# Negated scores, one fused join of a head's two maps, heads between scores, and the conv module's slots projected first

## The chip, the cores and the metric

The kernel runs as one program on one core of a Trainium2 chip. The metric is the device time of that core in microseconds (us), the median of several runs. In the profile's words PE is TensorE (PEld its weight loads), DVE is VectorE, ACT is ScalarE, POOL is GpSimd and SP is SyncE, whose queue issues the loads of weights.

## What is computed

256 tokens of width 1024 go through two layers of a first block and then through a second block (latent attention, pooling and two passes over 128 expert slots). The change lies in the mixer of the first block's two layers, of which this matters:

```python
for l in range(DEPTH):                      # 2 layers
    h = rms_norm(x, pre_mix_w[l])
    u = h @ w_in[l]
    (u_conv, dq, dk, dv, gqkv, gz, b_f, b_b, a_f, a_b) = jnp.split(u, offs, axis=-1)
    y_conv = conv_module(u_conv, ...)       # a * sigmoid(g), 31 taps, layer norm, silu
    y_diff = diff_attention(dq, dk, dv, ...)
    y_delta = gated_deltanet(gqkv, gz, b_f, b_b, a_f, a_b, ...)   # 3 taps, silu, chunks
    y = jnp.concatenate([y_conv, y_diff, y_delta], axis=-1) @ w_out[l]
    ...
# diff_attention: 6 heads, two maps each (12 maps), 128 queries x 256 keys twice
s = jnp.einsum("bqmd,bkmd->bmqk", q_blk, kf)
p = jax.nn.softmax(s - slopes[:, None, None] * dist, axis=-1)
a = p[:, :, 0] - lam * p[:, :, 1]
o = rms_norm(jnp.einsum("bhqk,bkhe->bqhe", a, vf), subln_w, eps=1e-5) * (1.0 - lambda_init)
```

## The kernel before

Each engine has one instruction stream, and semaphores tie them together. The order of a layer's mixer is written out by hand, in the same order in each engine's function: `pe_layer`, `dve_layer`, `act_layer` and `pool_layer`.

TensorE writes its results into four PSUM banks in rotation. The list in `layer_jobs` names every use of a bank and the engine that empties it. `J.give` on TensorE takes the next bank and waits until the job four places earlier has been read; `J.take` on the reader waits until the bank is filled; `J.evac` waits until a job has been read.

The weights come in slots of 1 MB through a ring of four, loaded by SyncE in the order in which TensorE uses them; `project(i, key)` multiplies slot 4 + i with the activations, 16 matmuls of 256 columns for each of a slot's two tiles of 128 channels. Before the change the order is: the untransposed slots ("zb", "dv"), the five "s" slots (the channels of the delta net's q, k and v; the fifth holds one tile), "cg" and "ca" (gate and value of the conv module), then small sums of the log decays ("gc", "gl", four "gr"), then "d" 0, the sums for the l2 norm ("l2"), "d" 1 and "d" 2 (q and k of the attention).

VectorE waits for the last "s" slot (evacuated by ScalarE) and runs the short convolution of three taps: nine TENSOR_SCALAR (L997) and eighteen SCALAR_TENSOR_TENSOR (L999) over 256 elements, all from SBUF to SBUF. Behind it in VectorE's queue stand the product for `cpad`, the conv module's padded input (L1008), the copy of "gc" and the four "gr". ScalarE waits for the short convolution (signal `sconv`), then applies silu and square, loads another table and reads "gl". GpSimd waits for the reading of "ca" and then works off the conv module's 31 taps, each a TENSOR_TENSOR multiply (L1416) and a TENSOR_TENSOR add (L1418) over 512 elements: 20 of them, then after the last head's output a square (`od2`), 3 taps, a reciprocal root, twelve scalings of keys and values, and the last 8 taps.

The scores follow: for each of 12 maps TensorE fills a bank (L559), VectorE adds the distance term (L1036), takes the maximum (L1039) and negates it (L1040), and ScalarE exponentiates with the row sums as a by-product (L1285). Only when all 12 are through VectorE come the six heads: reciprocal of the sums (L1048), factor lambda (L1049), scaling of the first map (L1051, two operations), adding the second map (L1054, two operations), and TensorE transposes the joined map ("ar", L593) and multiplies with v ("av", L570), ScalarE copying both out. The blocks "kk" and "qk" (L580) of the delta net are filled around the last head, and from there a long algebra of 64x64 blocks (L608) runs between TensorE, VectorE (L1067, L1070, L1082, L1086) and ScalarE.

Of the kernel before, what the change touches and what calls it, by code (L numbers as in the profile page):

```python
# [18 lines left out]
S = 256  # L19
TB = S // P  # L20
# [152 lines left out]
def layer_jobs():  # L173
    j = [(("h", i), "act" if i % 2 == 0 else "dve") for i in range(4)]
    j += [(("zb", tb), "act") for tb in range(TB)] + [(("dv", tb), "act") for tb in range(TB)]
    j += [(("s", i), "act") for i in range(5)]
    j += [("cg", "act"), ("ca", "dve"), ("gc", "dve"), ("gl", "act")]
    j += [(("gr", g), "dve") for g in range(GRP)] + [(("d", 0), "act")]
    j += [(("l2", i), "act") for i in range(3)]
    j += [(("d", i), "act") for i in range(1, 3)]  # L180
    j += [(("sc", m), "dve") for m in range(NMAP)]
    for h in range(DH + 1):
        if h >= DH - 1:
            j += [((("kk", "qk")[h - (DH - 1)], hp), "dve") for hp in range(2)]
# [157 lines left out]
def plan_memory(nc, ctx, k):  # L342
# [137 lines left out]
def pe_layer(k, pe, lay):  # L480
# [22 lines left out]
    def project(i, key):  # L503
# [8 lines left out]
        m.then_inc(J.filled, 1)  # L512
        rel.owe()

    for i in range(5):
        project(i, ("s", i))
    project(5, "cg")
    project(6, "ca")

    pe.wait_ge(k.const_loaded, 16)  # L520
    wait(k.g_ready)
# [30 lines left out]
    project(9, ("d", 2))  # L552

    J.evac(pe, ("d", 2), lay)
    for m_ in range(NMAP):
        b = J.give(pe, ("sc", m_), lay)
        r = (m_ % 4) * DD
        for qb in range(TB):
            m = pe.matmul(ps[b][:, qb * S:(qb + 1) * S], k.qkd[r:r + DD, m_ // 4, qb * P:(qb + 1) * P],  # L559
                          k.qkd[r:r + DD, 3 + m_ // 4, :], start=True, stop=True)  # L560
            if qb == 0:
                rel.pay(m)
        m.then_inc(J.filled, 1)
# [22 lines left out]
    for h in range(DH):  # L586
        if h == DH - 1:
            chunk_pairs("kk", 3)
        wait(k.attn_ready, h + 1)
        b = J.give(pe, ("ar", h), lay)  # L590
        for qb in range(TB):
            for kb in range(TB):
                m = pe.transpose(ps[b][:, kb * S + qb * P:kb * S + (qb + 1) * P],  # L593
                                 k.prob[:, 2 * h, qb, kb * P:(kb + 1) * P], c["ident"])
        m.then_inc(J.filled, 1)
        if h:
            attend(h - 1)
# [361 lines left out]
def dve_layer(k, v, lay):  # L959
# [28 lines left out]
    st.link(v.tensor_scalar(k.beta[:, :, :], k.beta[:, :, :], 1.0, None, ALU.add))  # L988
    st.link(v.reciprocal(k.beta[:, :, :], k.beta[:, :, :]))

    J.evac(v, ("s", 4), lay)
    for tap in range(3):
        for i in range(9):
# [8 lines left out]
            else:  # L1002
                st.done(m)
        st.settle()

    J.evac(v, "cg", lay)
    b = J.take(v, "dve", "ca", lay)
    v.tensor_tensor(k.cpad[:, :, PADC:PADC + S], shaped(ps[b][:, :], 2, S), k.csig[:, :, :], ALU.mult).then_inc(J.read["dve"], 1)  # L1008
# [24 lines left out]
    slopes = alibi(DH)  # L1033
    for m_ in range(NMAP):
        b = J.take(v, "dve", ("sc", m_), lay)
        v.scalar_tensor_tensor(k.prob[:, m_, :, :], k.dist[:, :, :], -slopes[m_ // 2], shaped(ps[b][:, :], TB, S),  # L1036
                               ALU.mult, ALU.add).then_inc(J.read["dve"], 1)
        J.evac(v, ("sc", m_), lay)
        st.link(v.tensor_reduce(k.mx[:, m_, :], k.prob[:, m_, :, :], AX.X, ALU.max))  # L1039
        v.tensor_scalar(k.mx[:, m_, :], k.mx[:, m_, :], -1.0, None, ALU.mult).then_inc(k.sc_max.sem, 1)  # L1040
    wait(k.gc_exp)
    v.tensor_tensor(k.beg[:, :, :], k.beta[:, :, :], k.eg[:, :, :], ALU.mult).then_inc(k.beg_ready.sem, 1)
# [3 lines left out]
    for h in range(DH):  # L1046
        wait(k.sc_exp, 2 * h + 2)
        st.link(v.reciprocal(k.ssum[:, 2 * h:2 * h + 2, :], k.ssum[:, 2 * h:2 * h + 2, :]))  # L1048
        st.link(v.tensor_scalar(k.ssum[:, 2 * h + 1, :], k.ssum[:, 2 * h + 1, :], k.lam[:, 5:6], None, ALU.mult))  # L1049
        for qb in range(TB):  # L1050
            st.done(v.tensor_scalar(k.prob[:, 2 * h, qb, :], k.prob[:, 2 * h, qb, :], k.ssum[:, 2 * h, qb:qb + 1], None, ALU.mult))  # L1051
        st.settle()
        for qb in range(TB):
            m = v.scalar_tensor_tensor(k.prob[:, 2 * h, qb, :], k.prob[:, 2 * h + 1, qb, :], k.ssum[:, 2 * h + 1, qb:qb + 1],  # L1054
                                       k.prob[:, 2 * h, qb, :], ALU.mult, ALU.add)
            st.done(m) if qb == 0 else m.then_inc(k.attn_ready.sem, 1)
    by_dir = lambda M, hp: M.rearrange("p (d m h) j -> p d m h j", d=2, h=2)[:, :, :, hp, :]
    for name, to, E in (("kk", k.A, k.EB), ("qk", k.AQ, k.E)):
        for hp in range(2):
# [159 lines left out]
def act_layer(k, a, lay):  # L1219
# [30 lines left out]
    a.activation(k.negA[:, :], k.row[:, R_ALOG:R_ALOG + 12], ACT.Exp).then_inc(k.gate_exp.sem, 1)  # L1250
    wait(k.lam_arg)
    a.activation(k.lam[:, 2:4], k.lam[:, 0:2], ACT.Exp).then_inc(k.lam_exp.sem, 1)
    for i in range(5):
        n = 1 if i == 4 else 2
        copy(("s", i), k.raw[:, 2 * i:2 * i + n, 1:S + 1], lambda t, n=n: shaped(t[:, 0:n * S], n, S))
    copy("cg", k.csig[:, :, :], lambda t: shaped(t[:, :], 2, S), ACT.Sigmoid)
    wait(k.sconv)
    sa.link(a.activation(k.sT[:, :, :], k.sT[:, :, :], ACT.Silu))
    a.activation(k.sq[:, :, :], k.sT[:, 0:6, :], ACT.Square).then_inc(k.sq_ready.sem, 1)
# [22 lines left out]
    for m_ in range(NMAP):  # L1282
        wait(k.sc_max, m_ + 1)
        for qb in range(TB):
            m = a.activation(k.prob[:, m_, qb, :], k.prob[:, m_, qb, :], ACT.Exp, bias=k.mx[:, m_, qb:qb + 1],  # L1285
                             accum_out=k.ssum[:, m_, qb:qb + 1])
            sa.done(m) if False else m.then_inc(k.sc_exp2.sem if qb == 0 else k.sc_exp.sem, 1)

    def out_head(h):
        copy(("av", h), k.od[:, :, h * HD:(h + 1) * HD], lambda t: shaped(t[:, 0:2 * HD], 2, HD))  # L1290

    for h in range(DH):
        copy(("ar", h), k.ATd[h % 2][:, :, :], lambda t: shaped(t[:, :], TB, S))
        if h:
            out_head(h - 1)
    out_head(DH - 1)
    def stack(key, M, g):
        copy(key, M[:, GH * g:GH * g + GH, :], lambda t: shaped(t[:, 0:BLOCKS], GH, CHUNK))
# [98 lines left out]
def pool_layer(k, p, lay):  # L1397
# [26 lines left out]
    x_rstd(1)  # L1424
    p.wait_ge(k.const_loaded, 16)
    J.evac(p, "ca", lay)
    conv_taps(range(0, 20))
    J.evac(p, ("av", DH - 1), lay)
    p.tensor_tensor(k.od2[:, :, :], k.od[:, :, :], k.od[:, :, :], ALU.mult).then_inc(k.od_sq.sem, 1)
    conv_taps(range(20, 23))  # L1430
    wait(k.od_ss)
    pool_rsqrt(k, p, sp, k.onorm[:, :], k.inv_hd, k.eps5, k.od_rstd)
    wait(k.beg_ready)
# [1 line left out]
    for dr in range(2):  # L1435
        for tb in range(TB):
            for src, dst, f in ((k.Kn, k.kbg, k.beg), (k.Kn, k.kdec, k.ekd), (k.Vn, k.vb, k.beta)):
# [3 lines left out]
                    m.then_inc(k.kv_scaled.sem, 1)  # L1441
                else:
                    sp.done(m)
    conv_taps(range(23, CONV_W))
    J.evac(p, ("ao", 3), lay)
    p.tensor_tensor(k.o2[:, :, :], k.o[:, :, :], k.o[:, :, :], ALU.mult).then_inc(k.o_sq.sem, 1)
    wait(k.o_ss)
# [1117 lines left out]
def layer_slots(i, l):  # L2565
# [80 lines left out]
```

## Time and profile before

| | us |
|---|---|
| median of 3 runs | 3168.43 |
| lowest, highest | 3165.46, 3171.89 |
| the profiled execution | 3174.81 |
| its span | 3172.8 |
| TensorE busy | 2939.2 (93%) |
| VectorE busy | 2045.8 (64%) |
| ScalarE busy | 1096.8 (35%) |
| GpSimd busy | 227.4 (7%) |
| mean granted TensorE clock | 0.948 of full |

The times are those of whole executions; the span is what the profiler saw between the first and the last instruction of one further execution. Busy shares are means over stages of very different kinds: the expert passes, which fill most of the span, have TensorE busy nearly throughout, and the two mixers, of some 300 us each, don't. All GpSimd work of note lies in the two mixers.

### The profile page before, as it was taken

How to read it: one execution, taken by the hardware profiler on the slowest of the kernel's cores; microseconds unless marked ns; L12 is line 12 of the kernel's file. 1: busy time of each engine (PE TensorE's matmuls, PEld its weight loads, DVE VectorE, ACT ScalarE, POOL GpSimd, SP SyncE). 2: the span in 40 equal slices, each digit the busy share in tenths (PEclk: the TensorE clock that was granted, in tenths of full speed). 3: DMA queues.
4: the chain of work that ended last, by engine and by line, in shares of the span. 5: the costliest groups of instructions: out<-in, count | busy, mean ns of one | idle time of the engine just before them, and what ended most of it. 6: DMA issues, size and time to landing. Idle time of an engine off the chain costs nothing.

```text
span 3172.8 us, 50021 instructions
## 1 busy us (share of the span) xinstructions
PE 2939.2 (93%) x19336; PEld 2496.4 (79%) x19340; DVE 2045.8 (64%) x3676; ACT 1096.8 (35%) x1741; POOL 227.4 (7%) x208
## 2 busy tenths in 40 slices
PE   8896999977799998989999999998898999999997
PEld 6684897867499745879899999885688989999986
DVE  1863885485388242599766666674289966666677
ACT  2321553241255230123444444441012344444443
POOL 0651000362100000000000000000000000000000
PEclk9797999977899998999999999998899999999999
DMA  5100884400388212442355555654353145445564
GB/s 208 65 17 13 321 327 148 173 15 15 145 328 302 90 50 97 169 153 79 136 183 185 185 185 185 221 199 151 133 173 131 68 174 181 182 184 184 185 239 152
DMA packets 77555, 502.31 MB, mean 158 GB/s; under 512 B 9072, under 2 KB 9456, under 8 KB 20592
## 3 DMA queue, kind: packets, MB, share of 16 engines
q1 hardware_dynamic: 71520, 481.72, 41.6%
q10 hardware_dynamic: 5904, 18.71, 1.6%
q8 instruction: 97, 1.59, 0.2%
q14 instruction: 34, 0.28, 0.0%
HBM read 487.82 MB, written 12.58 MB: 158 GB/s over the span
## 4 chain that ended last, share of the span: by engine, by line
PE 63%; DVE 9%; issue 1%; ACT 0%; DMA 0%; POOL 0%; DVEq 0%; ACTq 0%; POOLq 0%
PE bank L776 18%; PE bank L788 18%; PE bank L818 8%; PE bank L1814 4%; PE bank L1768 4%; PE bank L1823 4%; PE bank L1631 2%; PE bank L1651 1%; DVE sb L2039 1%; DVE sb L2032 1%; PE bank L1847 1%; DVE sb L2033 1%; DVE sb L2036 1%; DVE sb L2029 1%; DVE sb L2071 1%; DVE sb L2069 1%
## 5 line engine op out<-in xcount | busy, mean ns | idle before, releaser
L788 PE MATMUL bank<-peer_pass_high,peer_pass_hidden 128*128 128x512 f32 x1344 | 452.4, 398 | 0.0
L776 PE MATMUL bank<-peer_pass_high 128*128 128x256 f32 x1344 | 383.6, 285 | 13.8 <-DVE ring_r L863 13.8
L776 PE MATMUL bank<-peer_pass_high,ring_r 128*128 128x256 f32 x1344 | 385.8, 287 | 0.0
L776 PE MATMUL bank<-hT_r,peer_pass_high 128*128 128x256 f32 x1344 | 381.4, 284 | 0.0
L863 DVE TENSOR_TENSOR ring_r<-ring,peer_pass_high 128x1024 fp32r<-128x1024 f32 x168 | 205.8, 1225 | 194.1 <-ACT peer_pass_high L1356 194.1
L788 PEld LDWEIGHTS bank<-peer_pass_high,peer_pass_hidden 128*128 128x128 f32 x1344 | 253.9, 189 | 53.7
L776 PEld LDWEIGHTS bank<-peer_pass_high 128*128 128x128 f32 x1344 | 257.5, 192 | 22.7 <-issue 14.8
L1356 ACT ACTIVATE peer_pass_high<-ring 128x1024 fp32r<-128x1024 f32 x168 | 178.3, 1061 | 270.5 <-DMA ring<-in_experts 269.7
L788 PE MATMUL bank<-ring_r,peer_pass_hidden 128*128 128x512 f32 x672 | 267.4, 398 | 0.0
L776 PEld LDWEIGHTS bank<-hT_r,peer_pass_high 128*128 128x128 f32 x1344 | 257.9, 192 | 7.0
L776 PEld LDWEIGHTS bank<-peer_pass_high,ring_r 128*128 128x128 f32 x1344 | 257.4, 192 | 0.0
L1370 ACT ACTIVATE sb<-bank 128x256 f32<-128x256 f32 x232 | 89.4, 386 | 398.5 <-PE bank L776 398.5
L818 PE MATMUL bank<-peer_pass_high,peer_pass_hidden 128*128 128x512 f32 x704 | 225.0, 400 | 0.0
L867 DVE TENSOR_TENSOR ring_r<-ring,peer_pass_high 128x1024 fp32r<-128x1024 f32 x168 | 204.7, 1218 | 4.4 <-ACT peer_pass_high L1361 4.2
L1789 PE MATMUL bank<-sb,ring 128*128 128x256 f32 x896 | 193.7, 379 | 0.0
L1789 PEld LDWEIGHTS bank<-sb,ring 128*128 128x128 f32 x896 | 170.1, 190 | 23.0
L875 DVE TENSOR_TENSOR sb<-sb 128x256 f32<-128x256 f32 x168 | 104.7, 623 | 127.4 <-ACT sb L1370 127.4
L1361 ACT ACTIVATE peer_pass_high<-ring 128x1024 fp32r<-128x1024 f32 x168 | 175.7, 1046 | 7.9 <-PE bank L788 7.9
L788 PE MATMUL bank<-ff_high,ff_hidden 128*128 128x512 f32 x512 | 171.7, 397 | 2.2 <-DVE ff_hidden L872 2.2
L818 PEld LDWEIGHTS bank<-peer_pass_high,peer_pass_hidden 128*128 128x128 f32 x704 | 132.9, 189 | 32.7 <-issue 0.5
L2270 POOL TENSOR_SCALAR sb<-sb 128x2 f32<-128x2 f32 x4 | 1.9, 464 | 2120.1 <-DVE sb L1909 2120.1
L776 PE MATMUL bank<-ff_high 128*128 128x256 f32 x512 | 146.9, 287 | 5.8 <-DVE ring_r L863 5.8
(345 smaller groups left out, 5890.4 us busy)
## 6 DMA issues: line engine op xcount, KB each, us to landing
ring<-in_experts SPq DMA_DIRECT2D x256, 1024.0 KB, 4.8
ring<-in_w SPq DMA_DIRECT2D x139, 1024.0 KB, 4.9
sb<-in_w_mod SPq DMA_DIRECT2D x48, 1024.0 KB, 6.8
spill<-sb ACTq DMA_DIRECT2D x22, 512.0 KB, 6.5
sb<-spill SPq DMA_DIRECT2D x44, 256.0 KB, 5.1
sb<-in_ln ACTq DMA_DIRECT2D x8, 512.0 KB, 4.8
sb<-in_post ACTq DMA_DIRECT2D x4, 512.0 KB, 4.4
sb<-in_ctx SPq DMA_DIRECT2D x2, 1024.0 KB, 17.3
```

The lines of the kernel that those rows point to most:

```text
L776: m = pe.matmul(ps[u][:, 0:S], w, h[:, kt, :], start=(kt, i) == (0, 0), stop=(kt, i) == (KT - 1, 2))
L788: m = pe.matmul(ps[4 + 2 * tb + half][:, :], g[:, t], w, start=False, stop=False, skip_group_check=True)
L818: m = pe.matmul(ps[4 + 2 * tb + d][:, :], g[:, rows], w, start=False, stop=False, skip_group_check=True)
L863: v.tensor_tensor(k.ring_r[u][:, 0:D], k.ring[u][:, 0:D], X.uh[u % 2].bitcast(F32), ALU.subtract).then_inc(X.u_split, 1)
L867: v.tensor_tensor(k.ring_r[u][:, D:SLOT], k.ring[u][:, D:SLOT], X.vh[u % 2].bitcast(F32), ALU.subtract).then_inc(X.v_split, 1)
L875: v.tensor_tensor(X.g[u % 2], X.r[u % 2], factor(i, u), ALU.mult).then_inc(X.chain, 1)
L1356: a.activation(X.uh[u % 2], k.ring[u][:, 0:D], ACT.Copy).then_inc(X.u_high, 1)
L1361: a.activation(X.vh[u % 2], k.ring[u][:, D:SLOT], ACT.Copy).then_inc(X.v_high, 1)
L1768: m = pe.matmul(ps[b][:, kk * S:(kk + 1) * S], w[:, kk * D + kt * P:kk * D + (kt + 1) * P], k.hT[:, kt, :], start=kt == 0, stop=kt == KT - 1)
L1789: m = pe.matmul(ps[b][:, 0:S], w[:, (t % 2) * D + kt * P:(t % 2) * D + (kt + 1) * P], k.hT[:, kt, :], start=kt == 0, stop=kt == KT - 1)
L1814: m = pe.matmul(ps[g % 4][:, t * P:(t + 1) * P], k.hot[g % 2][:, 0, t, :], k.hot[g % 2][:, 1, t, :], start=True, stop=True)
L1823: m = pe.matmul(ps[b][:, 0:S], w[:, (t % 2) * D + kt * P:(t % 2) * D + (kt + 1) * P], k.hT[:, kt, :], start=kt == 0, stop=kt == KT - 1)
```

## The change

It makes four edits, in both layers.

1. Scores are kept negated: VectorE computes slope x distance minus the score and takes the minimum, which ScalarE uses as it is, with scale -1. The negation (L1040) is gone.
2. A head's maps are joined unscaled: the ratio of the two sums times lambda is made by one small fused operation, the first map isn't scaled, and the division by its sum is done where ScalarE copies the head's output out of the bank, in two operations in place of one.
3. The heads stand between the scores in all engines: six scores ahead on TensorE and ScalarE, four on VectorE, then a head and two more scores in turn.
4. The slots "cg" and "ca" are projected before the five "s" slots, and the weights are laid out in that order. GpSimd does all 31 taps in one run as soon as "ca" is read.

```diff
@@ layer_jobs
-    j += [(("s", i), "act") for i in range(5)]
-    j += [("cg", "act"), ("ca", "dve"), ("gc", "dve"), ("gl", "act")]
+    j += [("cg", "act"), ("ca", "dve")] + [(("s", i), "act") for i in range(5)]
+    j += [("gc", "dve"), ("gl", "act")]
...
-    j += [(("sc", m), "dve") for m in range(NMAP)]
+    j += [(("sc", m), "dve") for m in range(6)]
     for h in range(DH + 1):
         if h >= DH - 1:
             j += [((("kk", "qk")[h - (DH - 1)], hp), "dve") for hp in range(2)]
         j += [(("ar", h), "act")] * (h < DH) + [(("av", h - 1), "act")] * (h > 0)
+        j += [(("sc", m), "dve") for m in range(2 * h + 6, min(2 * h + 8, NMAP))]
@@ pe_layer
+    project(0, "cg")
+    project(1, "ca")
     for i in range(5):
-        project(i, ("s", i))
-    project(5, "cg")
-    project(6, "ca")
+        project(2 + i, ("s", i))
...
+    for m_ in range(6):
+        score(m_)
...
         if h:
             attend(h - 1)
+        for m_ in range(2 * h + 6, min(2 * h + 8, NMAP)):
+            score(m_)
@@ dve_layer
+    J.evac(v, "cg", lay)
+    b = J.take(v, "dve", "ca", lay)
+    v.tensor_tensor(k.cpad[...], shaped(ps[b][:, :], 2, S), k.csig[:, :, :], ALU.mult)...
+
     J.evac(v, ("s", 4), lay)
     for tap in range(3):
...
-    J.evac(v, "cg", lay)
-    b = J.take(v, "dve", "ca", lay)
-    v.tensor_tensor(k.cpad[...], ...)
...
-        v.scalar_tensor_tensor(k.prob[:, m_, :, :], k.dist[:, :, :], -slopes[m_ // 2], shaped(ps[b][:, :], TB, S),
-                               ALU.mult, ALU.add).then_inc(J.read["dve"], 1)
+        v.scalar_tensor_tensor(k.prob[:, m_, :, :], k.dist[:, :, :], slopes[m_ // 2], shaped(ps[b][:, :], TB, S),
+                               ALU.mult, ALU.subtract).then_inc(J.read["dve"], 1)
         J.evac(v, ("sc", m_), lay)
-        st.link(v.tensor_reduce(k.mx[:, m_, :], k.prob[:, m_, :, :], AX.X, ALU.max))
-        v.tensor_scalar(k.mx[:, m_, :], k.mx[:, m_, :], -1.0, None, ALU.mult).then_inc(k.sc_max.sem, 1)
+        v.tensor_reduce(k.mx[:, m_, :], k.prob[:, m_, :, :], AX.X, ALU.min).then_inc(k.sc_max.sem, 1)
...
-        st.link(v.reciprocal(k.ssum[...], k.ssum[...]))
-        st.link(v.tensor_scalar(k.ssum[:, 2 * h + 1, :], k.ssum[:, 2 * h + 1, :], k.lam[:, 5:6], None, ALU.mult))
-        for qb in range(TB):
-            st.done(v.tensor_scalar(k.prob[:, 2 * h, qb, :], k.prob[:, 2 * h, qb, :], k.ssum[:, 2 * h, qb:qb + 1], None, ALU.mult))
-        st.settle()
+        st.link(v.reciprocal(k.rsum[:, 2 * h:2 * h + 2, :], k.ssum[:, 2 * h:2 * h + 2, :]))
+        st.link(v.scalar_tensor_tensor(k.ssum[:, 2 * h + 1, :], k.rsum[:, 2 * h + 1, :], k.lam[:, 5:6], k.ssum[:, 2 * h, :],
+                                       ALU.mult, ALU.mult))
...
+    for m_ in range(4):
+        score(m_)
+    wait(k.gc_exp)
+    v.tensor_tensor(k.beg[:, :, :], k.beta[:, :, :], k.eg[:, :, :], ALU.mult).then_inc(k.beg_ready.sem, 1)
+    for h in range(DH):
+        head(h)
+        for m_ in range(2 * h + 4, min(2 * h + 6, NMAP)):
+            score(m_)
@@ act_layer
+    copy("cg", k.csig[:, :, :], lambda t: shaped(t[:, :], 2, S), ACT.Sigmoid)
     for i in range(5):
...
-    copy("cg", k.csig[:, :, :], lambda t: shaped(t[:, :], 2, S), ACT.Sigmoid)
...
+                m = a.activation(k.prob[:, m_, qb, :], k.prob[:, m_, qb, :], ACT.Exp, scale=-1.0, bias=k.mx[:, m_, qb:qb + 1],
+                                 accum_out=k.ssum[:, m_, qb:qb + 1])
...
+            m = a.activation(k.od[:, qb, h * HD:(h + 1) * HD], ps[b][:, qb * HD:(qb + 1) * HD], ACT.Copy,
+                             scale=k.rsum[:, 2 * h, qb:qb + 1])
...
+    exponentials(range(6))
     for h in range(DH):
         copy(("ar", h), k.ATd[h % 2][:, :, :], lambda t: shaped(t[:, :], TB, S))
         if h:
             out_head(h - 1)
+        exponentials(range(2 * h + 6, min(2 * h + 8, NMAP)))
@@ pool_layer
     J.evac(p, "ca", lay)
-    conv_taps(range(0, 20))
+    conv_taps(range(CONV_W))
     J.evac(p, ("av", DH - 1), lay)
     p.tensor_tensor(k.od2[:, :, :], k.od[:, :, :], k.od[:, :, :], ALU.mult).then_inc(k.od_sq.sem, 1)
-    conv_taps(range(20, 23))
...
-    conv_taps(range(23, CONV_W))
@@ layer_slots
-    pairs = [(0, 1), (2, 3), (4, 5), (6, 7), (8,), (11, 12), (9, 10), (13, 14), (15, 16), (17, 18)]
+    pairs = [(11, 12), (9, 10), (0, 1), (2, 3), (4, 5), (6, 7), (8,), (13, 14), (15, 16), (17, 18)]
```

## Rows read from the trace of the kernel before

**Rows 1.** Windows: busy us of PE, PEld, DVE, ACT, POOL; clock; DMA; layers 0, 1.

```profile
38.80:84.00 45.20, 45.18 (x211) 39.81 (x211) 10.70 (x32) 13.63 (x18) 0.00 (x0) 1.00 0.56 205
113.20:157.30 44.10, 29.48 (x149) 21.65 (x150) 37.56 (x76) 18.84 (x60) 22.13 (x19) 0.55 0.07 24
157.30:217.80 60.50, 55.89 (x1718) 54.04 (x1718) 48.03 (x64) 19.33 (x41) 46.09 (x38) 0.99 0.07 21
635.30:676.80 41.50, 26.88 (x149) 19.14 (x150) 37.57 (x77) 18.84 (x60) 22.14 (x19) 0.59 0.07 26
```

**Rows 2.** Timeline of TensorE, layer 0: start, us, line, operation, idle before.

```profile
38.82 45.16 PE L508 MATMUL bank<-sb,ring 128*128 128x256 f32 x208 [1.00 <-DMA ring<-in_w]
...
88.92 7.17 PE L508 MATMUL bank<-sb,ring 128*128 128x256 f32 x32
...
113.24 1.17 PE L559 MATMUL bank<-sb 32*128 32x256 f32 x16 [0.75 <-ACT sb L1267]
...
120.15 2.07 PE L559 MATMUL bank<-sb 32*128 32x256 f32 x4 [0.40 <-DVE sb L1036]
...
143.81 1.09 PE L593 MATMUL bank<-sb 128*128 128x128 f32 x4 [9.26 <-DVE sb L1054]
```

**Rows 3.** Timeline of ScalarE, after the short convolution of layer 0.

```profile
80.56 2.13 ACT L1258 ACTIVATE sb<-sb 128x2304 f32<-128x2304 f32 x1 [1.55 <-DVE sb L999]
...
84.22 1.28 ACT L1261 ACT_TABLE_LOAD   x1
```

**Rows 4.** Timeline of VectorE: the short convolution, the first score.

```profile
70.70 2.46 DVE L997 TENSOR_SCALAR sb<-sb 128x256 f32<-128x256 f32 x9 [26.56 <-ACT sb L1234]
73.19 7.34 DVE L999 SCALAR_TENSOR_TENSOR sb<-sb 128x256 f32<-128x256 f32 x18
...
114.47 0.69 DVE L1036 SCALAR_TENSOR_TENSOR sb<-sb,bank 128x512 f32<-128x512 f32 x1 [1.04 <-PE bank L559]
```

**Rows 5.** Timeline of GpSimd: first tap, and two later ones.

```profile
84.95 1.04 POOL L1416 TENSOR_TENSOR sb<-sb 128x512 f32<-128x512 f32 x1 [74.66 <-DVE sb L1008]
...
101.09 1.04 POOL L1416 TENSOR_TENSOR sb<-sb 128x512 f32<-128x512 f32 x1
...
103.56 1.04 POOL L1416 TENSOR_TENSOR sb<-sb 128x512 f32<-128x512 f32 x1
```

**Rows 6.** Groups of VectorE, 84 to 137 us: count, busy us, mean ns, idle.

```profile
L1040 DVE TENSOR_SCALAR sb<-sb 128x2 f32<-128x2 f32 x9 | 10.1, 1121 | 0.3
...
L1039 DVE TENSOR_REDUCE sb<-sb 128x2 f32<-128x512 f32 x9 | 6.2, 687 | 0.3
L1023 DVE TENSOR_TENSOR sb<-sb 128x384 f32<-128x384 f32 x4 | 5.8, 1507 | 0.0
...
L1029 DVE SCALAR_TENSOR_TENSOR sb<-sb 128x768 f32<-128x768 f32 x1 | 1.9, 1877 | 0.0
```

**Rows 7.** Groups of TensorE, 142 to 157 us.

```profile
L570 PE MATMUL bank<-sb 128*128 128x64 f32 x32 | 7.2, 408 | 0.0
L593 PE MATMUL bank<-sb 128*128 128x128 f32 x20 | 5.4, 425 | 10.1 <-DVE sb L1054 10.1
```

**Rows 8.** Timeline of VectorE: a late negation, one head of six.

```profile
138.11 0.17 DVE L1040 TENSOR_SCALAR sb<-sb 128x2 f32<-128x2 f32 x1
...
143.62 0.17 DVE L1048 RECIPROCAL sb<-sb 128x4 f32<-128x4 f32 x1
...
144.10 0.62 DVE L1051 TENSOR_SCALAR sb<-sb 128x256 f32<-128x256 f32 x2
144.75 0.88 DVE L1054 SCALAR_TENSOR_TENSOR sb<-sb 128x256 f32<-128x256 f32 x2
145.55 0.17 DVE L1048 RECIPROCAL sb<-sb 128x4 f32<-128x4 f32 x1
```

**Rows 9.** Groups of VectorE, 160 to 174 us, taps running.

```profile
L1067 DVE TENSOR_TENSOR sb<-sb 128x384 f32<-128x384 f32 x4 | 5.8, 1502 | 0.0
```

**Rows 10.** Groups of VectorE, 211.4 to 217 us, after the last tap.

```profile
L1086 DVE TENSOR_TENSOR sb<-sb 128x384 f32<-128x384 f32 x2 | 1.2, 623 | 0.0
```

More of the change, by code:

```diff
@@ L333 @@
 RCOLS = 153
-DVE_STEPS, POOL_STEPS, ACT_STEPS = 152, 86, 10
+DVE_STEPS, POOL_STEPS, ACT_STEPS = 128, 86, 10
 class Ctx:
@@ L421, in plan_memory @@
     k.ssum = b.take(NMAP, TB)
+    k.rsum = b.take(NMAP, TB)
     k.negA = b.take(12)
@@ L554, in pe_layer, with score @@
     J.evac(pe, ("d", 2), lay)
-    for m_ in range(NMAP):
+    def score(m_):
         b = J.give(pe, ("sc", m_), lay)
@@ L989, in dve_layer @@
     st.link(v.reciprocal(k.beta[:, :, :], k.beta[:, :, :]))
+    J.evac(v, "cg", lay)
+    b = J.take(v, "dve", "ca", lay)
+    v.tensor_tensor(k.cpad[:, :, PADC:PADC + S], shaped(ps[b][:, :], 2, S), k.csig[:, :, :], ALU.mult).then_inc(J.read["dve"], 1)
     J.evac(v, ("s", 4), lay)
@@ L1032, in dve_layer @@
     v.wait_ge(k.const_loaded, 16)
-    slopes = alibi(DH)
-    for m_ in range(NMAP):
-        b = J.take(v, "dve", ("sc", m_), lay)
-        v.scalar_tensor_tensor(k.prob[:, m_, :, :], k.dist[:, :, :], -slopes[m_ // 2], shaped(ps[b][:, :], TB, S),
-                               ALU.mult, ALU.add).then_inc(J.read["dve"], 1)
-        J.evac(v, ("sc", m_), lay)
-        st.link(v.tensor_reduce(k.mx[:, m_, :], k.prob[:, m_, :, :], AX.X, ALU.max))
-        v.tensor_scalar(k.mx[:, m_, :], k.mx[:, m_, :], -1.0, None, ALU.mult).then_inc(k.sc_max.sem, 1)
-    wait(k.gc_exp)
-    v.tensor_tensor(k.beg[:, :, :], k.beta[:, :, :], k.eg[:, :, :], ALU.mult).then_inc(k.beg_ready.sem, 1)
     wait(k.lam_exp)
@@ L1045, in dve_layer, with score, head @@
     st.link(v.tensor_tensor(k.lam[:, 5:6], k.lam[:, 4:5], k.row[:, R_INIT:R_INIT + 1], ALU.subtract))
-    for h in range(DH):
-        wait(k.sc_exp, 2 * h + 2)
-        st.link(v.reciprocal(k.ssum[:, 2 * h:2 * h + 2, :], k.ssum[:, 2 * h:2 * h + 2, :]))
-        st.link(v.tensor_scalar(k.ssum[:, 2 * h + 1, :], k.ssum[:, 2 * h + 1, :], k.lam[:, 5:6], None, ALU.mult))
-        for qb in range(TB):
-            st.done(v.tensor_scalar(k.prob[:, 2 * h, qb, :], k.prob[:, 2 * h, qb, :], k.ssum[:, 2 * h, qb:qb + 1], None, ALU.mult))
-        st.settle()
+    slopes = alibi(DH)
+    def score(m_):
+        b = J.take(v, "dve", ("sc", m_), lay)
+        v.scalar_tensor_tensor(k.prob[:, m_, :, :], k.dist[:, :, :], slopes[m_ // 2], shaped(ps[b][:, :], TB, S),
+                               ALU.mult, ALU.subtract).then_inc(J.read["dve"], 1)
+        J.evac(v, ("sc", m_), lay)
+        v.tensor_reduce(k.mx[:, m_, :], k.prob[:, m_, :, :], AX.X, ALU.min).then_inc(k.sc_max.sem, 1)
+    def head(h):
+        wait(k.sc_exp, 2 * h + 2)
+        st.link(v.reciprocal(k.rsum[:, 2 * h:2 * h + 2, :], k.ssum[:, 2 * h:2 * h + 2, :]))
+        st.link(v.scalar_tensor_tensor(k.ssum[:, 2 * h + 1, :], k.rsum[:, 2 * h + 1, :], k.lam[:, 5:6], k.ssum[:, 2 * h, :],
+                                       ALU.mult, ALU.mult))
         for qb in range(TB):
@@ L1281, in act_layer, with exponentials, out_head @@
     a.activation(k.ekd[:, :, :], k.ekd[:, :, :], ACT.Exp).then_inc(k.gc_exp.sem, 1)
-    for m_ in range(NMAP):
-        wait(k.sc_max, m_ + 1)
-        for qb in range(TB):
[L1285 to L1290, printed above, removed]
+    def exponentials(maps):
+        for m_ in maps:
+            wait(k.sc_max, m_ + 1)
+            for qb in range(TB):
+                m = a.activation(k.prob[:, m_, qb, :], k.prob[:, m_, qb, :], ACT.Exp, scale=-1.0, bias=k.mx[:, m_, qb:qb + 1],
+                                 accum_out=k.ssum[:, m_, qb:qb + 1])
+                m.then_inc(k.sc_exp2.sem if qb == 0 else k.sc_exp.sem, 1)
+    def out_head(h):
+        b = J.take(a, "act", ("av", h), lay)
+        for qb in range(TB):
+            m = a.activation(k.od[:, qb, h * HD:(h + 1) * HD], ps[b][:, qb * HD:(qb + 1) * HD], ACT.Copy,
+                             scale=k.rsum[:, 2 * h, qb:qb + 1])
+        m.then_inc(J.read["act"], 1)
+    exponentials(range(6))
     for h in range(DH):
```

1 line of the change is left out of this document (removed).

## The prediction

> **What bounds the kernel now.** I read the page first: the chain that ended last is mostly TensorE in the expert passes, which the change doesn't touch. So I went to the stretches of a layer's mixer, by windows of its stages, and asked in each which engine ends last. The windows in [rows 1] are those of layer 0, with the score stage of layer 1 below them. While the transposed slots are projected (38.8 to 84.0 us) TensorE is busy for all 45.2 us and VectorE for a quarter of them. From 113.2 to 157.3, the scores and heads, TensorE is busy 29.5 of 44.1 us, at half clock for most of it, and VectorE 37.6: VectorE leads, and TensorE follows it. From 157.3 to 217.8 TensorE is busy 55.9 of 60.5 us; whatever VectorE gains there can return at most the 4.6 us in which TensorE is idle. Then I took the timelines of TensorE, ScalarE and VectorE around the short convolution, and GpSimd's taps. The reader should see three things in them: the last "s" slot is in at 70 us and two more slots (64 matmuls) keep TensorE busy until 84.0, so all that VectorE does from 70.70 to 80.5 is hidden behind projections [rows 2, 4]; ScalarE's silu, square and table load that follow end at 85.5 and are nearly hidden too [rows 3]; and GpSimd doesn't begin its taps until 84.95, so that no tap runs beside the short convolution [rows 5].
>
> **The slots' order.** "cg" and "ca" are projected first. 208 matmuls take 45.16 us [rows 2], 0.217 each, so the 64 of these two slots are 13.9 us: the "s" slots come 13.9 us later, the end at 84.0 stays, and the number of loads, their size and their places in the ring stay as well. VectorE's short convolution starts at 70.7 + 13.9 = 84.6 us, with nothing of it hidden. In VectorE's queue stand behind it the copy of "gc" and the four "gr"; in ScalarE's queue stand behind the signal sconv the silu, the square, the table load and the read of "gl". TensorE has four banks in rotation: "gr" 2 can't be given before "gc" is read, nor "gr" 3 before "gl" is read, and behind "gr" 3 in TensorE's own queue stand "d" 0, the l2 sums, "d" 1, "d" 2 and every score. That is a new wait, of a few microseconds if the short convolution still took its 9.8 us (70.70 to 80.5, [rows 4]).
>
> It will not take 9.8, I think. With "ca" in at 38.8 + 13.9 = 52.7 us, the product and the handoff (under 1 us from the last projection, at 84.0, to the first tap, at 84.95, [rows 2, 5]) put the first tap at about 54 us. A tap is two operations and 2.47 us when nothing disturbs it (101.09 to 103.56, [rows 5]); by 84.6 about 12 of the 31 are done, and 38 operations are still to come. So the 27 VectorE operations run beside GpSimd. What that costs, the old order shows in other places. A TENSOR_SCALAR over two elements takes 1.12 us at the median of nine while taps run (0.17 once that stretch of taps is over, [rows 8]), and the loop of scores beside it has the period of a tap; four TENSOR_TENSOR over 384 elements with both inputs in SBUF take 5.8 us in a row, 1.45 each, against 0.62 for the same shape without taps; a 768-element SCALAR_TENSOR_TENSOR takes 1.88; but one over 512 elements that reads a bank takes 0.69 beside them, no more than its elements need [rows 4, 6, 10]. So an operation with two inputs in SBUF gets one turn for each operation of GpSimd, and so does a TENSOR_SCALAR from SBUF to SBUF. The short convolution is nine of the latter and 18 of the former. The nine: half a tap's period each, 1.24, as the two-element ones: 11.1 us. The 18 have 256 elements; 1.24 is the floor, 1.45 the row for 384 elements, and I take 1.40, nearer the larger one because alone they come every 0.41 us (7.34 / 18), two thirds of the larger one's 0.62 [rows 4, 10]: 25.2 us. Together 36.3 us in place of 9.8. The bounds are 33.5 (27 times 1.24) and 39.2 (27 times 1.45). If the nine were not held up, 11.1 would be 2.5 and the whole 27.7.
>
> The Trainium skill, "SBUF — State Buffer", section "Who interferes with whom", speaks against this edit: a VectorE instruction with two SBUF inputs, or in a two-port mode, and a GpSimd instruction that reads SBUF shut each other out for the whole instruction. With whole instructions excluded (half a tap, 1.24 us, plus 0.41 or 0.27) the short convolution would be 18 x 1.65 + 9 x 1.51 = 43.3 us by that section, as an estimate, against 36.3 by the rows.
>
> Now the path. The convolution ends at 84.6 + 36.3 = 120.9. ScalarE needs for silu and square 3.66 us (80.56 to 84.22) and 1.28 for the table load [rows 3], with handoffs 5.1, and reads "gl" at 126.0; "gr" 3 takes about 1 us, and "d" 0 starts at about 127.1 where it started at 88.92 [rows 2]: 38.2 later. TensorE has stood idle for over 30 us by then; after 9 idle microseconds before the heads its granted clock stayed at the lower level, with matmuls of a head at twice their later time: the whole stage of scores and heads has a mean clock of 0.55 of full [rows 1, 2]. Some 3 to 4 us of "d" 0 at 1.2 GHz cost half of that, 1.8 us. The slots after it are back to back as before, VectorE's reciprocal starts as late after the l2 sums as before, and the taps are over by then (12 + 13.5 by 120.9, the other 5.5 by about 134). So the scores start 40.0 us later in each layer. The lambda operations that are moved ahead of the scores (0.4 us) fall into the wait for "d" 2.
>
> **Scores and heads.** The change drops the 12 negations (1.12 us for nine of them, 0.17 for three) and the two 256-element scalings of each head (144.10 to 144.75, 0.65 us); the bank's SCALAR_TENSOR_TENSOR (0.69) and the reduction (0.69) stay, and so do the two that join the maps [rows 4, 6, 8]. On VectorE a score is then 1.42 us with its handoffs. A head is 1.93 now; without the 0.65 it is 1.27 (0.48 for the two small operations, as long with the fused one, and 0.79 for the two that join): 12 x 1.42 + 6 x 1.27 = 24.7 us if VectorE never waits. It will wait at times: TensorE at half clock needs for a head 1.8 us (L570: 7.2 / 4), 0.85 to 1.08 (L593: 5.4 / 5) and 2.07 for two scores in separate row strips [rows 2, 7], some 4.7 us to VectorE's 4.1. At full clock it needs about half. ScalarE's exponentials, two bank copies in place of one and the rest stay at about 3.3 us a head, its 18.9 busy of 44.1 us [rows 1] spread over the heads. So "kk" is filled 29 us after VectorE's first score, from 26.5 (VectorE alone) to 31 (TensorE at half clock). Before it was 42.8 in layer 0 (157.3 less 114.5, [rows 4]) and about 2.6 less in layer 1, where the clock came back sooner (41.5 against 44.1 us, [rows 1]). The gain is 13.8 and 11.2, mean 12.5 us a layer.
>
> **All taps at once.** Before, GpSimd's last 11 taps ran beside the block algebra, where four masks took 5.8 us and would take 2.5 at the 0.62 that the same shape has without taps [rows 9, 10]. With the taps gone by 134, VectorE is faster there, but TensorE is busy 55.9 of 60.5 us [rows 1], so the return is below 4.6; I take 3.0, leaving the waits for banks. The conv module's sums are first read by the column means that TensorE gives after the last chunk of the scan, and its wait there was over long before; having them earlier returns nothing, and nothing behind the taps in GpSimd's queue gets late.
>
> **The sum.** Per layer +40.0 - 12.5 - 3.0 = +24.5, twice +49. Work outside the mixers is unchanged. The profiled execution took 3174.8 us around a span of 3172.8, 6.4 above the median of 3168.4; its span should become about 3222, and the median 3168.4 + 49 = 3217.
>
> **Rivals.** *VectorE isn't held up by the taps in the short convolution* (chance 0.10; the other side). Speaking for it: no row shows just this shape beside a tap. Against it: [rows 6, 10]. Then the convolution ends at 94.4, "gl" is read at 99.5, "d" 0 starts 11.7 late plus 1.8 for the clock: per layer +13.5 - 12.5 - 3.0 = -2.0, a time of 3164, which is no change. It decides if the short convolution takes less than some 12 us. *Only the operations with two inputs are held up* (0.12): 8.6 us less in each layer, 3200. For it: two elements are a poor sample for 256. *Each operation waits out a whole one of GpSimd* (0.18): 39.2 (27 at the 1.45 of the row) to 43.3 us (whole operations one after the other, 1.24 plus 0.41 or 0.27), 3 to 7 more a layer, 3223 to 3231. For it: the 768-element operation's 1.88. *TensorE at half clock becomes the bound of the heads* (0.10), its two scores one after the other at 2.07 each instead of together, for three of the heads: 6 us more in each layer, 3229. Against it: the first four scores, in four strips, took 1.17 us together [rows 2]. The forecast itself has 0.50, with 3208 to 3228 as its own range.
>
> **How the numbers follow.** The range takes in all but the first rival: from 3200 less 3 us a layer for faster heads and tail, 3194, to 3229 with 3 us a layer for the clock and banks, 3235. A measurement of this kernel tells a change from none beyond about 0.2%, 6.3 us. The first rival, 0.10, lies within that mostly: 0.06 for the same, 0.04 for faster; the rest, with a little of a tail that gives back more than I allow, is slower: 0.90 in all, all of them more than 20 us above.
>
> **What would show it.** In the profile after: the first tap at about 54 us; the short convolution (L997, L999 before) with an operation every 1.2 to 1.45 us in place of every 0.27 and 0.41, in a stretch from 84.6 to about 121; TensorE idle from about 87.5 until past 120, with a few matmuls between; "d" 0 near 127; first score near 153 to 155; "kk" some 29 us later; no taps after 135; TensorE's idle time in the block algebra down from 4.6 us to 1 or 2. The prediction is wrong if L999 keeps its 0.41 us beside the taps, or if TensorE's wait for the "gc" and "gl" banks isn't there.

## The result, and the profile after

The changed kernel takes 3213.44 us (median of 4, 3205.2 to 3215.21) against 3170.16 us of the kernel before (median of 4): a ratio of 1.0127, interval 1.0112 to 1.0141, so 43 us slower. Forecast were 49 us more and 3217. One execution further below, of the version that beats both, took 3790.5 us at a mean granted clock of 0.727 where the others of its kernel had 0.95, and medians and ratios here leave it out.

Windows of the changed kernel's layer 0, the first, third and fourth beside those in [rows 1], and as the last the score stage of layer 1 (columns as there; second row: from TensorE's halt to its first matmul after it):

```profile
41.60:86.80 45.20, 45.19 (x211) 39.82 (x211) 1.63 (x6) 8.30 (x14) 28.26 (x25) 1.00 0.54 194
88.80:122.00 33.20, 1.62 (x51) 1.48 (x50) 33.09 (x28) 0.18 (x1) 31.16 (x27) 0.56 0.07 28
153.60:183.20 29.60, 23.21 (x149) 18.10 (x150) 22.91 (x49) 18.99 (x64) 0.00 (x0) 0.57 0.11 36
183.20:239.60 56.40, 54.88 (x1722) 53.82 (x1722) 38.70 (x64) 19.76 (x43) 17.44 (x16) 0.99 0.08 23
692.90:722.50 29.60, 23.21 (x149) 18.11 (x150) 22.91 (x49) 18.97 (x64) 0.00 (x0) 0.57 0.11 36
```

VectorE was busy 10.7 us of the projections before [rows 1] and is busy 1.6 now; the work hasn't gone, it stands in the second row, where VectorE and GpSimd are busy for nearly all of 33.2 us and TensorE for 1.6. The timelines of VectorE, TensorE, ScalarE and GpSimd in that stretch show where each engine stood:

```profile
87.23 11.26 DVE L1009 TENSOR_SCALAR sb<-sb 128x256 f32<-128x256 f32 x9 [30.71 <-ACT sb L1248]
98.52 23.27 DVE L1011 SCALAR_TENSOR_TENSOR sb<-sb 128x256 f32<-128x256 f32 x18
121.71 0.20 DVE L1019 COPY sb<-bank 128x48 f32<-128x48 f32 x1
```

```profile
88.76 1.61 PE L543 MATMUL bank<-sb 64*64 64x64 f32 x48
121.96 1.55 PE L543 MATMUL bank<-sb 64*64 64x64 f32 x24 [31.58 <-DVE sb L1019]
127.02 1.54 PE L543 MATMUL bank<-sb 64*64 64x64 f32 x24 [3.52 <-ACT sb L1275]
...
153.62 1.17 PE L562 MATMUL bank<-sb 32*128 32x256 f32 x16 [0.75 <-ACT sb L1281]
```

```profile
121.82 2.13 ACT L1272 ACTIVATE sb<-sb 128x2304 f32<-128x2304 f32 x1 [33.33 <-DVE sb L1011]
...
125.48 1.28 ACT L1275 ACT_TABLE_LOAD   x1
```

```profile
56.66 1.05 POOL L1438 TENSOR_TENSOR sb<-sb 128x512 f32<-128x512 f32 x1 [46.23 <-DVE sb L1001]
...
106.10 1.10 POOL L1438 TENSOR_TENSOR sb<-sb 128x512 f32<-128x512 f32 x1
107.28 1.32 POOL L1440 TENSOR_TENSOR sb<-sb 128x512 f32<-128x512 f32 x1
108.68 1.10 POOL L1438 TENSOR_TENSOR sb<-sb 128x512 f32<-128x512 f32 x1
...
133.80 1.46 POOL L1440 TENSOR_TENSOR sb<-sb 128x512 f32<-128x512 f32 x1
```

L1009 and L1011 are the short convolution, the 9.8 us of [rows 4]: the nine come every 1.25 us, the 18 every 1.29. Two of the latter fit one tap beside them, 106.10 to 108.68, 2.58 us where a tap alone takes 2.47 [rows 5]. What makes the operations so slow is tested below. TensorE waits 31.58 us for VectorE's copy of "gc" (L1019) and then, for "gr" 3, 3.52 us for ScalarE.

The layer cut at the same five events, in us, shows where the time went (from TensorE's timelines; "slots" begins at the first transposed slot, "kk" is its last matmul, "w" the first product behind the block algebra, "out" the output projection, and the last column ends at the transposes of the expert pass):

| | slots to scores | scores to kk | kk to w | w to out | out to transposes |
|---|---|---|---|---|---|
| before, layers 0, 1 | 74.4, 74.4 | 44.0, 41.4 | 60.6, 61.0 | 56.8, 58.9 | 45.0, 45.1 |
| after | 112.0, 112.0 | 29.6, 29.6 | 56.4, 57.1 | 55.4, 54.4 | 46.4, 46.6 |
| difference | +37.6, +37.6 | -14.4, -11.8 | -4.2, -3.9 | -1.4, -4.5 | +1.4, +1.5 |

That is +19.0 in layer 0 and +18.9 in layer 1, of 40.4 us between the two profiled executions (3174.8 and 3215.2). The untransposed slots of layer 0 took another 2 us longer in this execution (23.6 against 21.5), because the clock came up later, at 20.9 us against 14.8; until then their matmuls came every 0.68 us and not every 0.34.

### The profile page after: what moved, and what is told of

It is laid out like the page before. It is cut to its first block, busy times and chain, and to the rows that moved or that the text cites. A ratio compares the mean times of both kernels' runs of the same rounds, so it can differ in the third digit from the quotient of the medians.

```text
span 3213.4 us, 49985 instructions
## 1 busy us (share of the span) xinstructions
PE 2930.2 (91%) x19340; PEld 2493.0 (78%) x19340; DVE 2045.5 (64%) x3628; ACT 1097.2 (34%) x1753; POOL 220.2 (7%) x208
## 4 chain that ended last, share of the span: by engine, by line
PE 62%; DVE 9%; issue 1%; ACT 0%; DMA 0%; POOL 0%; DVEq 0%; ACTq 0%; POOLq 0%
PE bank L784 18%; PE bank L796 17%; PE bank L826 8%; PE bank L1834 4%; PE bank L1788 4%; PE bank L1843 4%; PE bank L1651 2%; PE bank L1671 1%; DVE sb L2059 1%; DVE sb L2052 1%; PE bank L1867 1%; DVE sb L2053 1%; DVE sb L2056 1%; DVE sb L2049 1%; DVE sb L2091 1%
## 5 line engine op out<-in xcount | busy, mean ns | idle before, releaser
L826 PEld LDWEIGHTS bank<-peer_pass_high,peer_pass_hidden 128*128 128x128 f32 x704 | 132.9, 189 | 33.2 <-DVE ring_r L940 0.5
L1195 DVE SCALAR_TENSOR_TENSOR sb<-sb 128x2048 f32<-128x2048 f32 x64 | 148.8, 2346 | 0.0
```

Of the source, the lines that this page charges most:

```text
L826: m = pe.matmul(ps[4 + 2 * tb + d][:, :], g[:, rows], w, start=False, stop=False, skip_group_check=True)
L1195: v.scalar_tensor_tensor(k.mod_sum[:, to, :], k.mod_in[u], k.cs[:, bass.ds(i + 8 * ctx, 1)], k.mod_sum[:, to, :], ALU.mult, ALU.add).then_ ...
```

## The experiments

Ten runs of nine kernels. "Before" beside each is the kernel before on the same chip in the same hours, 3174 to 3176 us there, a little more than above; so ratios are to be compared, not medians across chips.

### The scores' edits alone

```diff
 (changed kernel, with the slots in the old order and the taps as before)
-    j += [("cg", "act"), ("ca", "dve")] + [(("s", i), "act") for i in range(5)]
+    j += [(("s", i), "act") for i in range(5)] + [("cg", "act"), ("ca", "dve")]
...
-    conv_taps(range(CONV_W))
+    conv_taps(range(0, 20))        # then 20 to 22 and 23 to 30, as before
```

> Edits 1 to 3 alone: negated scores, fused join and heads between scores, with the slots and the taps in the order of before. My theory (the loss is the slots' order, the gain is the scores): from the first score to the filled kk blocks some 33 us in place of 44.0 and 41.4 in the two layers, a little more than the 29.6 of the changed kernel, because the first 20 taps run until about 135 us and the joins, with two inputs in SBUF, take turns with them. Median about 3150. Rival 1: the taps don't matter to the joins, 29.6 us, median about 3144. Rival 2: the scores' edits gain nothing in the old order (TensorE at half clock bounds them), about 3170.

Measured: 3165.52 us, ratio 0.9970 (0.9956 to 0.9984). Scores to kk took 36.0 and 37.2 us, 8.0 and 4.2 less than before. So the gain is there, and neither rival holds, but my 33 was too low by 3 to 4, and the median missed my 3150: 10 us less than before and not 18. The groups of VectorE from 114 to 151 us in this kernel:

```profile
L1059 DVE SCALAR_TENSOR_TENSOR sb<-sb 128x256 f32<-128x256 f32 x12 | 10.1, 884 | 0.2
...
L1048 DVE SCALAR_TENSOR_TENSOR sb<-sb,bank 128x512 f32<-128x512 f32 x12 | 8.2, 680 | 1.0 <-PE bank L562 0.9
L1056 DVE SCALAR_TENSOR_TENSOR sb<-sb 128x2 f32<-128x2 f32 x6 | 3.1, 522 | 0.2
```

The joins take 0.88 us on average (0.48 in the changed kernel, where no tap runs beside them) and even the two-element fused operation 0.52 against 0.22 in the changed kernel: the edits trade operations that waited for taps against others that do. The block algebra gave nothing back (60.9 and 61.3 us): its masks still ran beside taps, at 1.56 us each.

### The slots' order alone

```diff
 (kernel before)
-    for i in range(5):
-        project(i, ("s", i))
-    project(5, "cg")
-    project(6, "ca")
+    project(0, "cg")
+    project(1, "ca")
+    for i in range(5):
+        project(2 + i, ("s", i))
...
-    conv_taps(range(0, 20))
+    conv_taps(range(CONV_W))
...
 (cpad's product, the copies, the weights' layout and the later taps: as in the change)
```

> Edit 4 alone: cg and ca projected first and all 31 taps in one run, the old scores and heads. My theory: scores start 37.6 us later in each layer, the nine negations that stood behind taps cost 0.17 in place of 1.12 us (-8.6 a layer), the block algebra gives back 4: +25 a layer, median about 3220. Rival: the slow negations have another cause than taps beside them and stay: +33 a layer, median about 3237.

Measured: 3234.84 us, ratio 1.0201 (1.0178 to 1.0223), 59 us more than before; the expected 50 was 9 too low. Slots to scores took 112.2 and 112.0, as in the changed kernel; scores to kk 35.4 and 35.5, so the negations did speed up (all 12 at 0.17 us). What was missing is the block algebra: 60.6 and 61.1 us, nothing given back, although its masks ran at 0.87 us in place of 1.50. TensorE was at half clock for about its first 10 us there (see the section on the hardware).

### GpSimd pauses for the short convolution

```diff
 (changed kernel)
-    conv_taps(range(CONV_W))
+    conv_taps(range(0, 12))
+    wait(k.sconv)
+    conv_taps(range(12, CONV_W))
```

> The changed kernel with one wait more: GpSimd does 12 taps, waits for the short convolution to end (its signal sconv), then does the other 19. My theory (the short convolution is slow because it takes turns with the taps): it takes 9.8 us again in place of 34.5, scores start about 13.6 us later than before the change in place of 37.6, the later taps run beside the scores until about 146 us and cost the joins some 2 to 4 us a layer: median about 3173, from 3165 to 3178. Rival: the short convolution is slow for a reason other than the taps beside it (its place in the queue, the bank waits): it stays at 34.5 us and the median at about 3213 or above.

Measured: 3185.12 us, ratio 1.0034 (1.0018 to 1.0050). This is the cleanest of them, one wait more and no work less. VectorE's timeline in it, and GpSimd's:

```profile
87.15 2.46 DVE L1009 TENSOR_SCALAR sb<-sb 128x256 f32<-128x256 f32 x9 [30.71 <-ACT sb L1248]
89.64 7.34 DVE L1011 SCALAR_TENSOR_TENSOR sb<-sb 128x256 f32<-128x256 f32 x18
```

```profile
84.65 1.27 POOL L1440 TENSOR_TENSOR sb<-sb 128x512 f32<-128x512 f32 x1
97.13 1.05 POOL L1438 TENSOR_TENSOR sb<-sb 128x512 f32<-128x512 f32 x1 [11.20 <-DVE sb L1011]
```

The convolution is back to 9.8 us at the same place in the queue, and slots to scores take 88.0 and 87.9: 24 less than in the changed kernel, 13.6 more than before. The median missed my range of 3165 to 3178 above: scores to kk took 35.3 and 35.4, some 6 us more than without taps and not 2 to 4, since the later taps ran beside the joins (0.79 us each), and the block algebra took 60.7 and 60.8 us, some 4 more than in the changed kernel (see the section on the hardware).

### Tap operations of half the size

```diff
 (changed kernel)
-            sp.link(p.tensor_tensor(k.ctap[:, :, :], k.cpad[:, :, tap:tap + S], w, ALU.mult))
+            for i in range(2):
+                m = p.tensor_tensor(k.ctap[:, i, :], k.cpad[:, i, tap:tap + S], w[:, i, :], ALU.mult)
...
 (and the add in two halves likewise)
```

> The changed kernel with each tap operation of GpSimd cut into two of half the size (256 elements), 124 operations in place of 62. My theory (one turn of VectorE for each operation of GpSimd): a VectorE operation beside them comes every 0.7 to 0.85 us in place of 1.25 to 1.29, so the short convolution takes 19 to 23 us in place of 34.5 and the median is about 3185 to 3192. Rival (the two engines share the bandwidth of a port by elements, whatever the instructions' size): the short convolution stays at 34 us or above and the median at about 3213.

Measured: 3193.03 us, ratio 1.0060 (1.0037 to 1.0083). VectorE's timeline:

```profile
86.34 6.50 DVE L1009 TENSOR_SCALAR sb<-sb 128x256 f32<-128x256 f32 x9 [30.71 <-ACT sb L1248]
92.88 14.68 DVE L1011 SCALAR_TENSOR_TENSOR sb<-sb 128x256 f32<-128x256 f32 x18
```

21.2 us in place of 34.5, with the same elements moved by both engines; the median is 1 us above my range. So the wait goes by instructions and not by elements: what fits is that each VectorE operation waits out what GpSimd has begun, and a shorter one is over sooner.

### The log decays ahead of the short convolution

```diff
 (changed kernel: VectorE's gc and gr operations, and ScalarE's gl, moved up)
+    b = J.take(v, "dve", "gc", lay)
+    ...
     J.evac(v, ("s", 4), lay)
     for tap in range(3):
```

> The changed kernel with the reading of gc, gl and the four gr (VectorE's copies and ScalarE's exponential) put ahead of the short convolution. That takes the bank waits away; the taps still run beside the short convolution. My theory (the long convolution itself is late, and the l2 sums wait for it in any case): TensorE runs gr 2, gr 3 and d 0 early and then waits for the silu and square, which come some 8 us later than in the changed kernel because the gr operations stand ahead; d 1, d 2 and the scores start within 3 us of where they were, median 3208 to 3220. Rival (the waits for the banks of gc and gl are what costs): scores start about 12 us earlier in each layer, median about 3190.

Measured: 3220.18 us, ratio 1.0129 (1.0111 to 1.0146), no better than the changed kernel's 1.0127. Slots to scores took 111.2 in both layers. TensorE's timeline in it:

```profile
91.32 7.17 PE L510 MATMUL bank<-sb,ring 128*128 128x256 f32 x32
133.34 4.58 PE L551 MATMUL bank<-sb 128*128 128x512 f32 x6 [34.84 <-ACT sb L1275]
```

"d" 0 ran at once, and the wait moved whole to the l2 sums, with 34.84 us. The bank waits that the changed kernel's profile names (L1019) were the first gate in a row of two; taking it away is worth 0.8 us. The l2 sums did start 2.6 us earlier, counted from the first transposed slot, but ran at half clock (4.58 us against the changed kernel's 2.74).

### The short convolution slot by slot

```diff
 (changed kernel, dve_layer)
-    J.evac(v, ("s", 4), lay)
-    for tap in range(3):
-        for i in range(9):
+    for s_ in range(5):
+        J.evac(v, ("s", s_), lay)
+        for tap in range(3):
+            for i in range(2 * s_, min(2 * s_ + 2, 9)):
```

> The changed kernel with the short convolution done slot by slot as the s slots are read, in place of all 27 operations after the fifth. They still take turns with the taps (about 1.28 us each), but 24 of them now run while TensorE projects. My theory (a slow short convolution costs only by what of it is exposed): it ends some 11 us after the last slot instead of 34.5, scores start some 88 us after the first transposed slot in place of 112, the rest stays: median about 3168, from 3160 to 3176. Rival (the work of the two engines on the port is the bound, wherever it stands): no more than 10 us are gained in all, 3203 or above.

Measured: 3165.74 us, ratio 0.9963 (0.9943 to 0.9984), as expected. The operations are as slow as before (5.21 us for four), but the convolution ends at 97.2 us in place of 121.8, and slots to scores take 87.7 and 87.8. 27 slow operations cost only by the end that is exposed.

### The taps moved, nothing else

```diff
 (kernel before)
-    conv_taps(range(0, 20))
+    conv_taps(range(0, 11))
...
-    conv_taps(range(20, 23))
...
-    conv_taps(range(23, CONV_W))
+    conv_taps(range(11, CONV_W))
```

> The kernel before with nothing changed but the taps' places: 11 until the scores start, 20 after the scalings of keys and values. My theory: the negations no longer wait for a tap (0.17 in place of 1.12 us, nine of them), so first score to kk full takes 35.4 us in both layers in place of 44.0 and 41.4; 15 to 19 us in all, median about 3156 beside a before of about 3173. Rival (the scores are bound by TensorE at half clock, not by VectorE's negations): no change.

Measured: 3164.38 us, ratio 0.9955 (0.9938 to 0.9971). Scores to kk took 35.5 in both layers, as expected; the block algebra took 61.9 and 63.0, some 1 to 2 us more than before. So the gain was 12 us and not the 15 to 19 I had expected. The 20 taps behind the scalings are not the main reason: the next version has them too and takes 57.8 and 58.7, with TensorE at half clock for 1.5 us of it in place of 9.7 here.

### The version that beats both

The same move of the taps, with edits 1 to 3 and the slots in the old order.

```diff
 (changed kernel, with the slots in the old order)
-    conv_taps(range(CONV_W))
+    conv_taps(range(0, 11))
...
 (behind the scalings)
+    conv_taps(range(11, CONV_W))
```

> A version meant to beat both: edits 1 to 3 with the slots in the old order, and GpSimd's taps kept out of the scores and the block algebra's masks: 11 taps from 85 us until the scores start, the other 20 after the scalings of keys and values, from about 185 to 240 us, where the conv sums are first wanted at about 260. My theory: from first score to kk full 29.6 us in both layers (44.0 and 41.4 before), the masks fast as well: 12 to 15 us a layer in the scores and up to 3 in the algebra, median 3140 to 3150 beside a before of about 3173. Rival (20 late taps slow the block algebra and the scan instead, or come too late for the column means): no faster than the scores' edits alone, about -10 us.

Measured: 3144.64 us (3135.61 to 3147.55 in three executions), ratio 0.9879 (0.9852 to 0.9906). Then the same kernel once more, in more executions.

> The same kernel as e10_taps_late, timed again in more rounds because one execution of it had taken 3790.5 us at a clock of 0.727. My theory (that execution was a disturbance of the chip and not of the kernel): all rounds between 3130 and 3155, ratio near 0.99. Rival (the kernel itself falls into such a state at times): another execution above 3300.

Measured: 3146.39 us (3139.21 to 3147.71 in 5 executions), ratio 0.9916 (0.9902 to 0.9929): all five lie where I expected them. Windows of the first of the two runs, scores to kk and kk to w of layer 0:

```profile
113.40:143.30 29.90, 23.36 (x149) 18.18 (x150) 24.37 (x52) 18.92 (x64) 1.28 (x1) 0.57 0.10 36
143.30:201.00 57.70, 55.35 (x1718) 53.97 (x1718) 42.13 (x64) 19.78 (x43) 46.50 (x39) 0.99 0.08 22
```

The score stage is as short as in the changed kernel and starts 37.6 us earlier in the layer; the late taps end at 222.1 us, and TensorE's column means begin at 244.9. Both parts of the expectation held, the algebra's (57.8 and 58.7 us) included.

Last, the split after ten taps instead of eleven:

```diff
-    conv_taps(range(0, 11))
+    conv_taps(range(0, 10))
...
-    conv_taps(range(11, CONV_W))
+    conv_taps(range(10, CONV_W))
```

> As e10_taps_late with 10 taps ahead of the scores and 21 behind, so that no tap stands beside the two scalings of q and k and the small lambda operations before the first score. My theory: VectorE is free for the first score about 1 us sooner, but TensorE's first score (after d 2) is what it waits for, so at most 0.5 us a layer are gained: no measurable difference to e10_taps_late. Rival: VectorE is on the path there, 1.5 us a layer.

Measured: 3144.64 us, ratio 0.9912 (0.9898 to 0.9926), no difference to the 11 taps of 0.9916. Scores to kk took 29.6 in place of 29.9.

## Why the prediction was right, point by point

**The slots' order.** Right in mechanism and in place. The term was +40.0 us a layer and measured +37.6. Its first part, the short convolution at 36.3, measured 34.5, inside my bounds of 33.5 and 39.2: I took 1.40 us for an operation with two inputs, and it came every 1.29, nearer the floor of 1.24 than the 1.45 of the 384-element rows. The nine TENSOR_SCALAR were held up like the two-element ones (1.25 us against 1.12), so the second rival is off, and 34.5 is below the 39.2 where the third begins. The 1.8 us for the clock, an estimate for which I had shown no row, measured 0.8: "d" 0 took 7.98 us in place of 7.17. The pause shows the taps as the cause: the same operations at the same place need 9.8 us once no tap stands beside them. What is left then, +13.6 us, is the exposure of the convolution and of what follows it, which I had at 13.5 in the first rival. The Trainium skill's rule ("SBUF — State Buffer", "Who interferes with whom") has the pair of engines and the operations right. Taken as whole durations one after the other it gave 43.3 us, and the runs 34.5: an operation cost 0.88 (1.29 less 0.41) or 0.98 us (1.25 less 0.27) more than alone and not a whole 1.24. That it waits only for what GpSimd has left to do would explain this, and the scores' edits alone show one case of it: a one-element TENSOR_TENSOR (L1042) starts at 115.09 us, in the middle of a tap operation that runs from 114.43 to 116.07, and takes 0.99 us; the next one (L1043), at 116.12, is through in 0.16.

**The gate.** I named the banks of "gc" and "gl" as the wait. The profile names them too, but the run with the decays first shows that the l2 sums' wait for the square would have held TensorE nearly as long, to within 0.8 us at the scores. The size of the term hardly depended on it.

**Scores and heads.** 29 us to kk from VectorE's first score were forecast; it was 28.3 (154.86 to 183.2). The gain, 13.8 and 11.2 forecast, was 14.4 and 11.8. TensorE at half clock held VectorE up only twice (0.91 and 0.67 us before the fifth and sixth pair of scores), since it fills two scores at once in 2.08 us; so the fourth rival is off.

**The block algebra.** 3.0 us forecast, 4.2 and 3.9 measured, but this is the term that was right for less than its reason. TensorE's idle time there fell from 4.6 to 1.5 us, which is the part that faster masks return; where the other 1 us comes from stays open. In the slots' order alone and in the pause the masks were as fast, and kk to w took 60.6 to 61.1: TensorE came out of the scores at half clock and stayed there for about 10 us of it. So the term is -4 with the masks fast, and between 0 and +4 on top for the clock, a part that I had left out and that happened to be 0 here. That was luck.

**The sum.** +24.5 a layer forecast. The three terms measured give +19.0 and +21.9 (37.6 - 14.4 - 4.2 and 37.6 - 11.8 - 3.9), and the scan and the output projection, where the work is the same, 0.0 and -3.0 on top. Between w and the output projection TensorE was at half clock for 41 and 45 us before, and for 35 and 31 after, which is the likely reason; no run tests it. Medians: +43 against +49.

**The edits' shares.** The scores' edits gain 0.3% in the old order, and the slots' order costs 2.0%; together they cost 1.3%, not 1.7%. The stages say where the difference lies. In the scores the parts add up nearly (13.4 us a layer gained by the two, 13.1 by the whole). It is the block algebra, which neither part shortens: the scores' edits alone leave its masks beside taps, the slots' order alone leaves TensorE at half clock for 10 us of it, and only together does it give back 4 us a layer, 8 of the some 13 us between 1.3 and 1.7%. The rest is open.

## What to carry to other kernels

Before a GpSimd stretch is moved, look at what VectorE will run beside it: here an operation with two inputs in SBUF, or a TENSOR_SCALAR from SBUF to SBUF, took in the mean 0.8 to 1.1 us more beside 512-element taps than alone, whether it had 2 elements or 768, so count VectorE's operations and not their elements; put the taps where VectorE reads banks, or where it idles, and not beside its critical chain. Work that is hidden behind projections costs nothing until it is exposed; where it must follow late inputs, do it piece by piece as they arrive. And a wait that the profile names can be the first of two: check what the engine would wait for next before taking it away.

## What the runs showed of the hardware

- The waits of VectorE for GpSimd go by instruction: with 512-element taps 1.25 to 1.29 us for a VectorE operation of 256 elements, with 256-element taps 0.72 (6.50 / 9) and 0.82 (14.68 / 18), without taps 0.27 and 0.41. A TENSOR_TENSOR over 768 elements took 2.02 us beside taps (the scores' edits alone, L1038) and 0.95 without. Not each one waits: one that falls between two operations of GpSimd is done in 0.16 (L1043, above). GpSimd is slowed little, 2.58 us a tap in place of 2.47, and with the halved operations 3.23 in place of 2.75. An operation with one input in SBUF and the other in a bank isn't held up: 0.68 us with taps and without (L1048).
- The granted clock explains what I had no row for. It came back at the end of the heads at 158 us in layer 0 of the kernel before, 1 us behind kk, but some 10 us behind kk in the pause and the slots' order alone (windows of 4 us: 0.61 at 172 to 176, kk at 165; 0.68 at 194 to 198, kk at 187). The halved taps show its price within one execution: in layer 0 it came back 9.9 us behind kk and in layer 1 1.1 us. kk to w of the two, the same work with VectorE just as busy:

```profile
170.40:230.90 60.50, 58.94 (x1719) 57.64 (x1718) 38.61 (x64) 19.75 (x43) 17.28 (x16) 0.92 0.07 21
701.50:758.50 57.00, 54.95 (x1718) 53.70 (x1718) 38.62 (x64) 19.76 (x43) 17.43 (x16) 0.99 0.07 23
```

  TensorE is busy 4.0 us longer, and the stage takes 3.5 longer. What decides when the clock comes back was not tested. Executions of one kernel differ too: the kernel before at a mean clock of 0.954 took 3166.33 us and at 0.946 3184.2, a spread of 18 us with no instruction changed.
- TensorE at half clock filled two score banks in one 2.08 us (from 162.69 and twice more in layer 0), with the two maps in different strips of 32 rows; before the change each took 2.07 by itself [rows 2].
